# Eight in place of four of the 22 up-projection pairs of a layer computed as seven block products, twice in a layer two of them one behind the other

## The reference

```python
h = rmsnorm(x, p["ffn_norm"][layer])
up = h @ p["w_up"][layer]                      # 1024 -> 2 * 2816
c, fb = causal_dwconv(up, ffn_bufs[layer], p["ffn_conv_w"][layer], p["ffn_conv_b"][layer])   # 3 taps
x = x + (jax.nn.silu(c[..., :D_FF]) * c[..., D_FF:]) @ p["w_down"][layer]                  # 2816 -> 1024
```

## Time and profile before

| | us |
|---|---|
| median of 3 runs | 1167.91 |
| lowest, highest | 1167.72, 1168.47 |
| the profiled execution's own time | 1167.32 |
| its span, first to last instruction | 1165.6 |
| PE busy | 1149.0 (99%) |
| PEld busy | 1128.6 (97%) |
| DVE busy | 822.6 (71%) |
| POOL busy | 733.2 (63%) |
| ACT busy | 580.4 (50%) |
| mean granted TensorE clock | 0.998 |

### The profile page before, as it was taken

How to read it: one execution, slowest core, us unless ns; L and a number is a source line. 1 busy time by engine, 2 the same in 40 slices (tenths; PEclk the granted TensorE clock), 3 DMA queues, 4 the chain that set the end, 5 groups by cost and what they waited for, 6 DMA issues and landing times. The chain is left out here.

```text
span 1165.6 us, 21999 instructions
## 1 busy us (share of the span) xinstructions
PE 1149.0 (99%) x8442; PEld 1128.6 (97%) x8442; DVE 822.6 (71%) x1574; ACT 580.4 (50%) x1113; POOL 733.2 (63%) x779
## 2 busy tenths in 40 slices
PE   8999999999999999999999999999999999999997
PEld 8887999999999999999999999999999999999997
DVE  5999768878677867775614644388686778677655
ACT  7475555544554555443613533366346545644543
POOL 3986344459868985872664324334698679768633
PEclk9999999999999999999999999999999999999999
DMA  6311242213421423141422222322042213222312
GB/s 232 116 57 35 68 145 85 89 28 94 141 65 44 148 73 91 55 136 51 148 85 90 68 69 76 120 76 65 28 147 90 80 60 116 73 92 81 119 52 82
DMA packets 35688, 104.02 MB, mean 89 GB/s; under 512 B 5104, under 2 KB 7152, under 8 KB 35568
## 3 DMA queue, kind: packets, MB, share of 16 engines
q1 hardware_dynamic: 31504, 98.92, 26.6%
q10 hardware_dynamic: 4080, 3.69, 1.1%
HBM read 98.29 MB, written 4.79 MB: 88 GB/s over the span
## 5 line engine op out<-in xcount | busy, mean ns | idle before, releaser
L590 PE MATMUL psum<-x_hi,w_hi 128*128 128x288 f32 x1564 | 338.6, 298 | 1.3 <-POOL w_lo L1660 1.3
L590 PE MATMUL psum<-x_lo,w_hi 128*128 128x288 f32 x1564 | 335.6, 296 | 0.0
L590 PE MATMUL psum<-x_hi,w_lo 128*128 128x288 f32 x1564 | 335.5, 296 | 0.0
L1660 POOL TENSOR_TENSOR w_lo<-w_raw,w_hi 128x1024 fp32r<-128x1024 f32 (+1 forms) x84 | 182.3, 2176 | 186.7 <-ACT w_hi L1037 186.7
L590 PEld LDWEIGHTS psum<-x_hi,w_hi 128*128 128x128 f32 x1564 | 252.7, 189 | 3.6 <-POOL w_lo L1660 1.6
L590 PEld LDWEIGHTS psum<-x_hi,w_lo 128*128 128x128 f32 x1564 | 252.5, 188 | 0.0
L590 PEld LDWEIGHTS psum<-x_lo,w_hi 128*128 128x128 f32 x1564 | 252.5, 188 | 0.0
L2404 DVE SCALAR_TENSOR_TENSOR psum<-arena,params,psum 128x608 f32<-128x608 f32 x176 | 150.4, 854 | 58.5 <-ACT psum L1416 55.3
L1802 POOL TENSOR_TENSOR w_lo<-arena,w_hi 128x384 fp32r<-128x384 f32 x120 | 130.9, 1110 | 47.8 <-ACT w_hi L1327 47.8
L835 PE MATMUL psum<-block_hi,w_lo 128*128 128x288 f32 x504 | 149.3, 296 | 0.0
L835 PE MATMUL psum<-block_hi,w_hi 128*128 128x288 f32 x504 | 149.2, 296 | 0.0
(11 more groups left out here) (270 smaller groups left out, 2246.4 us busy)
## 6 DMA issues: line engine op xcount, KB each, us to landing
w_raw<-in_w_up SPq DMA_DIRECT2D x44, 512.0 KB, 3.6
arena<-in_w_up SPq DMA_DIRECT2D x44, 512.0 KB, 4.2
arena<-in_w_down SPq DMA_DIRECT2D x24, 384.0 KB, 3.6
w_raw<-in_w_down SPq DMA_DIRECT2D x24, 384.0 KB, 3.2
w_raw<-in_w_in_c SPq DMA_DIRECT2D x16, 512.0 KB, 3.6
w_raw<-in_w_in_ab SPq DMA_DIRECT2D x11, 512.0 KB, 3.5
w_raw<-in_w_out_ab SPq DMA_DIRECT2D x16, 256.0 KB, 2.7
w_raw<-in_w_out_c SPq DMA_DIRECT2D x8, 512.0 KB, 3.6
```

The lines of the kernel that those rows point to most:

```text
L590: last = nc.tensor.matmul(PS[:, 2 * (q % 2 if slot is None else slot) + half, 0:HALF], w[q][:, k * P:(k + 1) * P], r[:, r_at, half * HALF: ...
L1660: nc.gpsimd.tensor_tensor(w_lo[slot][:, 0:nk * P], raws[RAW_SLOT[RAW[u]]][:, 0:nk * P], w_hi[slot][:, 0:nk * P].bitcast(F32), ALU.subtract ...
```

## The change

One line, the kinds of the pairs. It holds for both layers.

```diff
     GROUPS = ((0, 6), (6, 6), (12, 6), (18, KF - 18))
-    PATTERN = ("PPPPPP", "PPSPSP", "PPSPSP", "PPPP")
+    PATTERN = ("PPPPSS", "PPSPSS", "PPSPSP", "PPSP")
     PB = state_pool.shape[2]
```

## The result

The changed kernel took 1214.91 us (median of 4 runs, 1214.62 to 1215.23), the kernel before 1167.82 in the same comparison. The ratio is 1.0404, with a 95% interval of 1.0392 to 1.0416: 4% slower. The span grew from 1165.6 to 1212.5 us, by 46.9.

A forecast was written before the change was run, and what follows sets the result against it. TensorE, busy 99% of the span, was taken as the bound. A layer's 5.6 + 6.65 + 2 x 2.2 - 1.56 gave +30.2 for both, the clock +7.0: span 1202.8, time 1205 us, 3.2% slower, range 1190 to 1217.

The forecast's parts named there:

- Step 1 and 2: In (1,4) before (1,5): GpSimd's added sum ends at 915.5, ScalarE copies its weights first, hidden blocks begin 2.9 us late.
- Step 3: Same hand-over: VectorE's R4 weight sum, 0.69 us, goes behind its last split; emptying A22's bank comes 3.35 us late.
- Step 4: Same hand-over: bank copy follows R4's weight copy; TensorE goes on at 929.5, 7.1 us late; place costs 5.6 us net.
- (0,4) to (0,5): First S entered late, emptying 2.7 us behind the matmuls, then a hand-over as at (1,4): +6.65 us without clock.
- (3,2): New S pair between two P pairs: nothing waits, so it saves its 1.56 us in full in each layer.
- The down-projection's wait: Behind each second S, four weight copies delay the hidden blocks; TensorE waits 2.2 us, bounds 0 and 4.
- The clock: Clock falls in the four 6.7 us gaps of second S pairs: net 1.75 us each, +7.0, bounds 0 to 9.6.
- the 2.2: Work lost per gap: 0.44 of a low clock lasting 4.5 to 5.5 us, read from matmuls at the program's start.
- That the clock stays up: Rival, chance 0.20: no clock fall in the gaps; 1198 us, between 1190 and 1198.5.
- The worse case: Rival, chance 0.14: GpSimd doesn't catch up in the four down-projections, matmuls wait 2 to 3 us more each: 1215 to 1222.
- The milder one: Rival, chance 0.10: GpSimd's sum doesn't hold ScalarE, each hand-over is 3.7 us late, clock unaffected: 1176 us.
- The faster one: Rival, chance 0.04: the second S's bank copy is never late, so the full 12.5 us is saved: 1155.4 us.

The follow-up runs named there:

- the run with six S pairs: Changed kernel with (0,5) and (1,5) as P again, leaving six S pairs a layer, none behind another: 1171.12 us, ratio 1.0029.
- the run with a late single S: Kernel before, with the S at (1,4) moved to (1,5) in each layer, right before the last P pair of a group: 1175.64 us, ratio 1.0068.
- the run with 28 and 9 added matmuls: Changed kernel with unused matmuls of ones added, 28 in every S behind an S and 9 in the down-projection behind it: 1203.56 us, ratio 1.0307.
- the down-projection's order: Changed kernel; before the down-projection ScalarE copies two of its four weight pieces ahead of the hidden blocks, the other two after: 1206.62 us, ratio 1.0335.
- all three orders: Changed kernel with hidden blocks first, second S's first bank copy early, and the down-projection's weight copies split around the hidden blocks: 1193.09 us, ratio 1.0215.
- the early copy: Changed kernel with the second S's first bank copy (A11) on ScalarE ahead of the first S's silu: 1206.4 us, ratio 1.0334.
- both edits: Changed kernel with hidden blocks ahead of the weights that wait for GpSimd's sum, and the second S's first bank copy early: 1201.55 us, ratio 1.0291.

## Why the prediction was right, and what it mis-sized

1205 was predicted, 3.2% slower, and 1214.9 measured, within 1190 to 1217. The sign and the mechanism were right, and the time was 10 us short.

- **Step 1 and 2, GpSimd's sum at the head of ScalarE's queue**: right. (1,4) starts 36.52 us later here (its first bank copy is at 946.73 for 910.21). With that the copy was forecast for 952.07 and came at 952.08, the hidden blocks for 952.62 and came at 952.62, the last split for 958.94 and came at 958.96. Without the cause the gap shrinks (the run with the hidden blocks first), though by half of what it should, because the second sum then holds the queue. As an account of this kernel the step holds; as a forecast of a mend it would have been too simple.
- **Step 3, VectorE's sum**: 1.00 us in place of the 0.69 counted, 0.3 late.
- **Step 4**: TensorE, forecast to go on at 966.0, went on at 966.40, after a gap of 6.72 (6.7 forecast). The start of the gap was late by as much, since A22 waited 0.6 us in (1,4) for R3's bank copy, which stands behind the weights that wait for the second sum; no step had that.
- **(0,4) to (0,5)**: 17.3 us for 17.7. VectorE's sum in (0,3) took the 0.68 us that were counted. In the traces of all nine other kernels with this sum in this place it took 1.8, so this term had some luck.
- **(3,2)**: 1.56 a layer in full. Confirmed here and in the run with six S pairs.
- **The down-projection's wait**: 2.31 for 2.2, and caused as said; two runs show it.
- **The clock**: the mis-sized term. The text had it fall "in each gap", four times, and counted 1.75 net, +7.0. Behind the gaps of 6.7 us it cost 1.4 to 2.0, 1.8 on the mean, against the 2.2 counted. But it fell eight times. The wait of 2.3 us, which the prediction had itself forecast, was not asked about. There TensorE is busy 35.30 us for 33.54, 1.76 more a time and 7.0 in all, of which 0.23 a time also stands where the clock stays up (33.77, in the run with a late single S). The 0.45 that was to return in the same wait did not, 1.8 in all, and the wait itself is 0.11 longer than counted, 0.4 in all. Together 9.2, which is 16.2 less the 7.0 predicted there. By spans and gaps: the gaps sum to 42.5 us, less 12.5 saved is +30.0, for 30.2 forecast. The rest is 16.9, forecast as 7.0. Some 13 of it are the clock's, by an estimate: 29.0 us of low clock lie behind the eight waits, and 0.44 of the work is lost in them. What is left is mostly some 0.2 for each new start of TensorE behind a wait, as the 0.23 above, and the 0.6 elsewhere.
- **Where the 2.2 came from**: a misreading that did no harm, by luck. The four matmuls at 5.55 at the program's start were taken for slow ones, at 0.24 us each, and so the low clock for 4.5 to 5.5 us long. But the third of them waited for ScalarE's weights:

```profile
6.13 0.30 PEld L659 LDWEIGHTS psum<-x_hi,w_hi 128*128 128x128 f32 x2 [0.32 <-ACT w_hi L1115]
```

  The matmuls of ones before them show when the clock rose: one begins every 0.21 us up to 4.2, and every 0.11 from there on, so the low clock stood for 3.1 us of work, and by that row 1.4 us would have been counted. In the changed kernel it stood for 6.83 us at each long gap, and the part behind the gap was 3.1 to 4.3 us.

The rivals. That the clock stays up is refuted by the windows and by the run with 28 and 9 added matmuls. The worse case (1215 to 1222) had its time nearly met, but not its cause: no wait of line 835 is longer than 2.3 us, and its cause is the order on ScalarE. The milder one fell with step 2. The faster one fell, and with it, as a forecast of the whole, the rule of the Trainium skill beside it ("Perfetto Trace Analysis", section "Identifying the Most-Contended Engine"), to optimize the engine with the highest occupancy first: TensorE stood at 97% by its weight loads and a cut of its work made it slower, because the cut was paid for in GpSimd's sums at a place where ScalarE could not go on without them. Where nothing waited, at (3,2), the cut gave its 1.56 us.

What stays open is which of the short waits bring the clock down, and why the port goes to VectorE at (0,4) of the changed kernel, in both layers, and to GpSimd in all nine other kernels with the sum in this place.

## What to carry to other kernels

When work is moved to a spare engine, its mean share says little: follow the in-order queue of whoever takes its result, and see what stands behind that instruction. Ask of every wait that you forecast, short ones too, whether the clock falls behind it: here that cost 1.5 us behind a wait of 2.3. And price the places of a change apart: here two of the four new S pairs of a layer cost 44 us, one was worth nothing even when mended, and one gave 3 us.

## What was not expected of the hardware

- **The clock behind short waits.** After 2.3 us of standing still the granted clock was 0.50 for 3.41 us in four of four down-projections of the changed kernel and in one of two of the run with a single late S; after 2.4 us at the entry of (0,4) in two of two in the runs with no second S and with the down-projection's order, in none of two in the run with all three orders, and in one of two in each of the six others with this entry, which makes 10 of 18. After 1.1 us it fell in none of four, and after 1.3 in none of two. After 6.7 it fell in four of four. The length alone does not decide: after 1.8 us it fell in two of two down-projections (all three orders), and after 3.0 in one of three with the early copy and in two of two with both edits.
- **One port for two engines.** VectorE's sum of 128x512 took 0.68 or 1.81 us, and GpSimd's subtraction beside it 1.85 or 1.28, by which of them was held, though both start within 0.02 us. S2 of (0,4) came 1.1 us later by it, and some 1.6 more were lost where the clock followed.
- **A matmul of ones in float32**, 128x128, takes 0.22 us, recorded as two of 0.11. The kernel before shows it too: its 12 such matmuls stand as 24 records.
